# Seventeen gate/up tile pairs as seven 256-column block products instead of eight

## The reference, cut to what matters

```python
hf = rms_norm(x, norm_ffn[l])                              # 512 tokens x 1024
gate, up = jnp.split(hf @ w_ffn_in[l], 2, axis=-1)         # 1024 -> 2 x 2816
x = x + (jax.nn.silu(gate) * up) @ w_ffn_out[l]            # 2816 -> 1024
return rms_norm(x, norm_final)
```

## Time and profile before

| what | us |
|---|---|
| median of 3 runs | 1576.23 (1576.15 to 1577.49) |
| profiled execution, first to last instruction (span) | 1574.7 |
| so around the span, by the median | 1.5 |
| TensorE busy | 1565.2 (99%) |
| VectorE busy | 913.5 (58%) |
| ScalarE busy | 641.9 (41%) |
| GpSimd busy | 68.1 (4%) |
| granted TensorE clock, mean | 0.999 |

### The profile page before, as it was taken

The page is one execution under the profiler, slowest core; times in us unless marked ns, Lnnn a source line. Parts: engine busy times, 40 slices in busy tenths (PEclk is TensorE's granted clock), DMA queues, the critical chain, the costliest instruction groups (busy, mean ns, idle before and its releaser), DMA issues.

```text
span 1574.7 us, 19003 instructions
## 1 busy us (share of the span) xinstructions
PE 1565.2 (99%) x7372; PEld 1293.9 (82%) x7372; DVE 913.5 (58%) x1353; ACT 641.9 (41%) x1001; POOL 68.1 (4%) x58
## 2 busy tenths in 40 slices
PE   9999999999999999999999999999999999999998
PEld 7877777788888888888888888898888888888887
DVE  6776878666645445357787445455655544434435
ACT  5455766643222222255454334343444332222314
POOL 0000000020000000040000010010001000000002
PEclk9999999999999999999999999999999999999999
DMA  5433232343232323222221242344122332332222
GB/s 191 123 104 100 82 95 74 101 140 94 94 107 91 96 94 107 82 95 96 81 67 60 75 134 87 113 133 135 60 94 94 108 98 95 94 107 94 94 84 77
DMA packets 48522, 155.64 MB, mean 99 GB/s; under 512 B 6064, under 2 KB 7472, under 8 KB 48304
## 3 DMA queue, kind: packets, MB, share of 16 engines
q1 hardware_dynamic: 48128, 153.90, 31.0%
q10 hardware_dynamic: 304, 0.52, 0.1%
HBM read 148.11 MB, written 2.10 MB: 95 GB/s over the span
## 4 chain that ended last, share of the span: by engine, by line
PE 98%; DVE 1%; ACT 0%; DMA 0%; issue 0%; SPq 0%; DVEq 0%; ACTq 0%
PE G L1010 85%; PE SC L1010 4%; PE O L1010 2%; PE TP L1010 2%; PE M L1010 2%; PE TP L1361 1%; PE TP L1305 1%; DMA RAW<-in_va 0%; PE TP L1410 0%; DVE WL L1919 0%; ACT WH L1448 0%; DVE MGl L1919 0%; DVE RAW L2479 0%; DVE T L2193 0%; PE M L1185 0%
## 5 line engine op out<-in xcount | busy, mean ns | idle before, releaser
L1010 PE MATMUL G<-XGh,WH 128*128 128x512 f32 x1248 | 492.6, 395 | 0.0
L1010 PE MATMUL G<-XGh,WL 128*128 128x512 f32 x1248 | 486.3, 390 | 0.0
L1010 PE MATMUL G<-XGl,WH 128*128 128x512 f32 x1248 | 485.9, 389 | 0.0
L1919 DVE TENSOR_TENSOR WL<-RAW,WH 128x1024 fp32r<-128x1024 f32 (+3 forms) x281 | 337.8, 1203 | 190.8 <-ACT WH L1448 190.2
L1448 ACT ACTIVATE WH<-RAW 128x1024 fp32r<-128x1024 f32 (+3 forms) x281 | 283.8, 1011 | 185.0 <-PE G L1010 173.6
L1010 PEld LDWEIGHTS G<-XGh,WH 128*128 128x128 f32 x1248 | 234.3, 188 | 54.5 <-issue 6.2
L1010 PEld LDWEIGHTS G<-XGh,WL 128*128 128x128 f32 x1248 | 234.2, 188 | 49.8
L1010 PEld LDWEIGHTS G<-XGl,WH 128*128 128x128 f32 x1248 | 234.5, 188 | 46.4
L1010 PE MATMUL G<-MGh,WH 128*128 128x512 f32 x400 | 155.9, 390 | 0.0
L1010 PE MATMUL G<-MGl,WH 128*128 128x512 f32 x400 | 155.6, 389 | 0.0
L1010 PE MATMUL G<-MGh,WL 128*128 128x512 f32 x400 | 155.6, 389 | 0.0
(11 more groups left out here) (317 smaller groups left out, 1796.9 us busy)
## 6 DMA issues: line engine op xcount, KB each, us to landing
RAW<-in_up SPq DMA_DIRECT2D x32, 512.0 KB, 3.5
RAW<-in_dn SPq DMA_DIRECT2D x32, 512.0 KB, 3.5
RAW<-in_fg SPq DMA_DIRECT2D x22, 512.0 KB, 3.5
RAW<-in_fu SPq DMA_DIRECT2D x22, 512.0 KB, 3.5
RAW<-in_g SPq DMA_DIRECT2D x16, 512.0 KB, 3.6
RAW<-in_f SPq DMA_DIRECT2D x16, 512.0 KB, 3.5
X<-in_x SPq DMA_DIRECT2D x16, 256.0 KB, 4.1
RAW<-in_q SPq DMA_DIRECT2D x8, 512.0 KB, 3.6
```

Source lines behind the costliest of these rows:

```text
L1010: return e.matmul(dst, st, mv, start=start, stop=stop, skip_group_check=True)
L1919: return e.tensor_tensor(dst, src, hi.bitcast(F32), ALU.subtract)
```

## The change: what it does

**The block scheme.** For 17 of the 22 pairs (f = 5 to 15 and 16 to 21) gate and up are no longer two units. The pair is a product of a 2 x 2 block matrix of weights (input features 0 to 511 and 512 to 1023; gate and up) with a 2 x 2 block matrix of activations (the same halves of the features; tokens 0 to 255 and 256 to 511). Done plainly that is eight block products; done by Winograd's form of Strassen's scheme it is seven, at the price of four sums of weight blocks, four sums of activation blocks and a chain of sums of the products. Each block product is 4 chunks x 3 matmuls = 12 matmuls of 256 columns. The seven left operands are, in their order, `t1` = b11 + b12, `t2` = t1 + b22, `b11`, `t3` = b12 + b22, `b21`, `b22`, `t4` = t2 + b21.

**Weights.** The work is now counted in items, each 128x512 in hi and lo. A plain unit is two items, a pair by sevens is seven. There are 10 slots for items (the six halves of `WH`/`WL` and `WTh`/`WTl`), and items are prepared 6 ahead (`AHEAD`). VectorE makes the four weight sums (`tile_sum`) from what plain DMAs have loaded: `fg` of the pair into `RAW[f % 2]`, the two halves of `fu` into a `T` tile and a half of `RAW[2]` (`fetch`).

**Activations.** While pairs 0 to 4 still run plainly (`DIRECT`), VectorE multiplies `X` by gain and `RB` (step `h`), makes the four sums of halves (`s13`, `s2`, `s4`), and hi and lo of the sums go to `QK` (`s_hi`, `s_lo`), those of the activations to `Vh`, `Vl` (`a_hi`, `a_lo`), for each kt = 0 to 3.

**Results.** The seven products go to half banks of `O`, `M`, `TP` and `SC`; products 4, 5 and 6 (counted from 0) are added by TensorE onto the banks of 2, 0 and 3. ScalarE copies product 2 out (`one_out`), VectorE subtracts (`w_less`, `v_less`, `c22`, `c12`, `c21`), ScalarE applies Silu to the two gate halves (`c11`, `silu`), VectorE multiplies (`z_mul`), and hi and lo follow (`z_hi`, `z_lo`). Hidden tiles 8 to 15 now go to `XGh`, `XGl`.

The diff, cut to its core (the unused option of splitting on GpSimd also goes):

```diff
+DIRECT = 5
+SLOTS, AHEAD = 10, 6
+SUM_AT = (0, 1, 2, 5)
...
+    for f in range(DIRECT):
+        t += plain("fg", f, 1024) + plain("fu", f, 1024)
+    t += [("st", f, j, S) for f in range(DIRECT, 16) for j in range(7)]
+    for n in range(8):
+        t += plain("f0", n, 1024)
+    t += [("st", f, j, S) for f in range(16, 22) for j in range(7)]
...
+            if name == "st" and part == 0:
+                side = n % 2
+                behind = self.item_of["st", n - 2, 6] + 1 if ("st", n - 2, 6) in self.item_of else 0
+                new = n - 2 < DIRECT or n in (16, 17)
+                out.append(("sums", n, 2, max(behind, held.get(2, 0)) if new else behind))
+                out.append(("pair", n, side, max(behind, held.get(side, 0))))
...
+    def prepare(self, upto):
+        while self.rounded < min(upto, len(self.items)):
+            name, f, j, _ = self.items[self.rounded]
+            if name == "st" and j in SUM_AT:
+                if (f, j) == (DIRECT, 0):
+                    self.settle(self.rounded)
+                self.put("tile_sum", f, SUM_AT.index(j))
+            self.put("item_hi", self.rounded)
+            self.rounded += 1
+    def settle(self, upto):
+        while self.rest < min(upto, self.rounded):
+            self.put("item_lo", self.rest)
+            self.rest += 1
+            self.fetch()
+    def item(self, name, n, part):
+        q = self.item_of[name, n, part]
+        self.prepare(q + AHEAD + 1)
+        self.settle(q + AHEAD)
+        return q
...
+    def seven(self, f):
+        for j in range(7):
+            self.tick()
+            if j == 0:
+                for n, kind in ((3, "one_out"), (3, "w_less"), (3, "v_less"), (4, "c22"), (5, "c11"), (6, "c12"), (7, "c21"),
+                                (8, "silu"), (9, "z_mul"), (10, "z_hi"), (11, "z_lo")):
+                    self.later(n, kind, f)
+            self.put("seventh", f, j, self.item("st", f, j))
...
     def ffn(self):
...
+        for f in range(DIRECT):
             if f == 0:
...
+                for kt in range(4):
+                    for kind in ("h", "s13", "s2", "s4"):
+                        self.later(3 + 3 * kt, kind, kt)
+                    self.later(4 + 3 * kt, "s_hi", kt)
+                    self.later(4 + 3 * kt, "s_lo", kt)
+                    self.later(5 + 3 * kt, "a_hi", kt)
+                    self.later(5 + 3 * kt, "a_lo", kt)
+            self.pair(f)
+        for f in range(DIRECT, 16):
+            self.seven(f)
+        self.drain()
+        self.residuals("f0", range(8))
...
+                elif kind == "seventh":
...
+                    bank = (OM[n % 2], TP[:, 0, :], SC[:, n % 2, :], TP[:, 1, :], SC[:, n % 2, :], OM[n % 2], TP[:, 1, :])[j]
...
+                    elif j == 4:
+                        e.wait_ge(seven_act, SEVEN_ACT["one_out", pairs[n]])
+                    elif j == 5:
+                        e.wait_ge(seven_dve, SEVEN_DVE["v_less", pairs[n]])
+                    else:
+                        e.wait_ge(seven_dve, SEVEN_DVE["c22", pairs[n]])
+                    e.wait_ge(i_hi, q + 1)
+                    for kt in range(4):
+                        at = slice(kt * P, (kt + 1) * P)
+                        hi, lo = left_of[j](kt)
...
+                        mm(bank, wh[:, at], hi, start=(kt == 0 and j < 4))
+                        mm(bank, wh[:, at], lo)
+                        if kt == 0:
+                            e.wait_ge(i_lo, q + 1)
+                        t = mm(bank, wl[:, at], hi, stop=(kt == 3))
+                    t.then_inc(i_done, 1)
...
+                elif kind == "w_less":
...
+                    e.wait_ge(seven_act, SEVEN_ACT["one_out", f])
+                    e.wait_ge(i_done, taken("st", f, 1))
+                    e.tensor_tensor(W_LESS, TP[:, 0, 0:HALF_S], ONE_OUT, ALU.subtract).then_inc(seven_dve, 1)
```

More of the change, by code:

```diff
@@ L143, in __init__ @@
         self.taken, self.split, self.loaded = 0, 0, 0
+        self.items = tail()
+        self.item_of = {(name, n, part): q for q, (name, n, part, _) in enumerate(self.items)}
+        self.rounded, self.rest, self.fetched = 0, 0, 0
+        self.fetches, self.pairs = self.tail_loads(), [f for f in range(22) if ("st", f, 0) in self.item_of]
         self.chains, self.emitted = [], set()
@@ L191, in drain, with tail_loads @@
             self.tick()
+    def tail_loads(self):
+        out, held, n_plain, last_pair = [], {}, 0, 0
+        for q, (name, n, part, _) in enumerate(self.items):
+            if name == "st" and part == 0:
[4 more added lines that the diff above has]
+                out.append(("pair", n, side, max(behind, held.get(side, 0))))
+                held[side] = q + 7
+                last_pair = q + 7
+            elif name != "st" and part == 0:
+                third = (len(self.units) + n_plain) % NRAW if name in ("fg", "fu") else n % NRAW
+                out.append((name, n, third, max(held.get(third, 0), last_pair if third == 2 else 0)))
+                held[third] = q + 2
+                n_plain += 1
+        return out
     def load(self):
@@ L205, in take @@
         assert self.units[u][:2] == (name, i), (self.units[u], name, i)
-        while self.split < min(u + ahead, len(self.units)):
+        while self.split < u + ahead:
             self.split_one()
@@ L235, in gemm @@
             self.pool_product(beside, 1)
-        while self.split < min(u + NW, len(self.units)):
+        while self.split < u + NW:
             self.split_one()
@@ L581, in half_gemm @@
         if half == 0:
[L582 to L585, removed]
+            self.item("f2", n, 1)
+        self.put("mm_half", n, g, half)
         self.put(*step)
@@ L630, in ffn @@
         assert self.taken == len(self.units)
+        assert self.rest == len(self.items) and self.fetched == len(self.fetches)
     def tally(self, *kinds, each=1, but=()):
@@ L912, in program, with taken @@
         s_silu, u_done, ff_hi, ff_lo = sem("s_silu"), sem("u_done"), sem("ff_hi"), sem("ff_lo")
-        FU = tally("fu")
+        FU = {step[1]: n for step, n in tally("fu", "z_mul").items()}
+        i_hi, i_lo, i_done = sem("i_hi"), sem("i_lo"), sem("i_done")
+        d_b12, d_b22 = d_x[0:2], d_x[2:4]
+        X_LOAD = 32
+        prep_act, prep_dve, seven_act, seven_dve, t_sum = (sem(n) for n in (
+            "prep_act", "prep_dve", "seven_act", "seven_dve", "t_sum"))
+        PREP_ACT, PREP_DVE = tally("s_hi", "a_hi"), tally("h", "s13", "s2", "s4", "s_lo", "a_lo")
+        SEVEN_ACT, SEVEN_DVE = tally("one_out", "c11", "silu"), tally("w_less", "v_less", "c22", "c12", "c21")
+        TURN7 = {f: k for k, f in enumerate(pairs)}
+        RAW_LOADS, n = {}, [sum(1 for v in range(len(units)) if v % NRAW == third) for third in range(NRAW)]
+        for i, (name, _, third, _) in enumerate(fetches):
+            if name != "sums":
+                n[third] += 1
+                RAW_LOADS[name, fetches[i][1]] = n[third]
+        def taken(name, n, part=1):
+            return item_of[name, n, part] + 1
         fh_done, fh_sq, fh_acc, out_done = sem("fh_done"), sem("fh_sq"), sem("fh_acc"), sem("out_done")
@@ L1883, in _ @@
                 kind, arg = step[0], step[1:]
[L1884 to L1891 removed]
+                if kind == "sq" and arg[1] > 0 and arg not in ADDS:
                     acc, sqs = STAT[arg[0]]
@@ L1936, in _ @@
                 kind, arg = step[0], step[1:]
-                if kind == "split" and lo_of[arg[0]][0] is w_lo_dve:
+                if kind == "split":
                     v = arg[0]
```

416 lines of the change are left out of this document (351 added, 65 removed).

## The result

| | before | after |
|---|---|---|
| median of 8 runs, us | 1576.22 | 1580.45 |
| lowest to highest, us | 1575.54 to 1577.49 | 1579.59 to 1581.15 |
| profiled execution: its span, us | 1574.7 | 1578.3 (its time 1580.13) |
| mean granted TensorE clock | 0.998 to 0.999 | 0.996 to 0.997 |

The ratio is 1.0026, with a 95% interval of 1.0016 to 1.0037: the change makes the kernel slower by 4.2 us, a little more than the 0.2% that can be told here. The forecast was 1577.0, called no change that can be told, with a range of 1565 to 1588: the time lies in the range, 3.4 us above the forecast, and on the slower side of what was called no change.

A forecast was written before the change was run, and what follows sets the result against it. TensorE, busy for 99% of the span, was taken to bound the kernel. From 1574.7, minus 14.0 saved, plus 13.8 preparation and 1.0 steady part, gave 1575.5; with 1.5 around the span 1577.0, range 1565 to 1588.

The forecast's parts named there:

- TensorE's term: Matmuls of the 17 pairs by sevens: 10.06 us a pair instead of 10.88, saving 14.0 us.
- The steady part: VectorE's 18 instructions per round by sevens just fit under TensorE's 10.06 us; 1 us lost over 17 pairs.
- the rival of VectorE's pace: Rounds by sevens: waits stretch VectorE's 18 instructions to 10.5 us, giving 1583.5 us; chance 0.22.
- that of the full duration: VectorE instructions cost their full shown durations: 11.0 us a pair, 21 in the preparation, 1599 us; chance 0.05.
- The preparation: VectorE's queue from pair 0 to pair 5's `v_less`: 51.8 us plus 13.9 of waits, TensorE loses 13.8.
- the lower bound of 4 us: Preparation in pairs 0 to 5: only the round trips of the product's lo part remain, a loss of 4.
- the rival of a hidden preparation: Preparation in pairs 0 to 5 is mostly hidden and costs some 4 us, giving 1566; chance 0.22.
- the 14 us of idle time that were to show it: Sign in the trace: TensorE idle between about 1226 and 1280 for some 14 us.
- slower matmuls have 1.7 us of slack at product 5: Pair 4 stalls may lower TensorE's clock, but 1.7 us of slack at pair 5's product 5 absorbs slower matmuls.
- The rival built on it (1581): Clock falls in the preparation's stalls: 10 us at half speed beyond the slack, up to 5 more, 1581; chance 0.06.
- while VectorE is on time: Condition on ScalarE's hand-overs in a round by sevens: `one_out`, `v_less` and `c22` meet their deadlines if VectorE is on time.
- no cost taken: Second block's preparation beside `f0`, block ends and the tail were priced at nothing.

The follow-up runs named there:

- e1: Changed kernel with the last two plain units' raw buffer thirds swapped, so the load ahead of `t1` is issued earlier; 1575.66 us.
- e2: Changed kernel with ScalarE's `s_hi` of kt = 2 and `a_hi` of kt = 3 ahead of the Silus of pairs 2 and 3; 1577.22 us.
- e3: Changed kernel with the preparation's eight lo parts (`s_lo`, `a_lo`) computed on 64 columns instead of 1024, the rest left out; 1574.04 us.
- e4: Changed kernel with ScalarE's rounding of the next tile of `f0` and `f1` behind `one_out` of pairs 15 and 21; 1579.07 us.
- e9: Changed kernel with `one_out` of pair 5 ahead of the rounding of pair 6's `t2` on ScalarE; 1580.78 us.
- e11: As e10, seven plain pairs with `one_out`, `w_less` and `v_less` moved earlier, but preparation steps every 5 ticks; 1566.95 us.
- e6: Changed kernel with seven plain pairs, preparation steps every 6 ticks, the early load and e4's order at the block ends; 1567.74 us.
- e7: Changed kernel with six plain pairs, preparation steps every 4 ticks, the early load and e4's order at the block ends; 1569.11 us.
- e8: Changed kernel with eight plain pairs, preparation steps every 6 ticks and e4's order at the block ends; 1567.21 us.
- e10: e6 with, for the first pair by sevens, `one_out` ahead of the next `t2` rounding and `w_less`, `v_less` ahead of the next `t3`; 1567.03 us.
- e12: e7 with `one_out`, `w_less` and `v_less` of the first pair by sevens moved earlier as in e10; 1568.75 us.
- e5: Changed kernel with the edits of e1, e2 and e4 together; 1571.32 us.

## Why the prediction came out as it did

**TensorE's term was right.** Block products take 1.44 us and rounds 10.08, against 10.06. 17 pairs save 17 x (10.88 - 10.08) = 13.6 us instead of 14.0. That narrow matmuls eat two fifths of "one product less in eight" could be read in the earlier trace rows.

**The steady part was right, with no loss instead of 1 us.** VectorE's instructions of 512 columns start 0.60 us apart, `t1`, `t2` and `z_mul` with their waits among them. From VectorE's timeline of the changed kernel:

```profile
1285.46 0.68 DVE L2814 TENSOR_TENSOR T<-RAW,T 128x512 f32<-128x512 f32 x1
1286.06 0.69 DVE L2239 TENSOR_TENSOR WTl<-F,WTh 128x512 fp32r<-128x512 f32 x1
1286.66 0.68 DVE L2818 TENSOR_TENSOR F<-T,RAW 128x512 f32<-128x512 f32 x1
```

Waits that are already met cost nothing in this stream. This refutes the rival of VectorE's pace (10.5 us a round) and that of the full duration (11.0). The section of the Trainium skill that the second of these drew on ("VectorE: DVE Perf Modes", section "The DRAIN you can't avoid") goes on to say that an instruction which is not held starts earlier. That half of it agrees with the 0.60 us here; the rival had taken the other.

**The preparation: the queue was right, what TensorE does beside it was not.** The trace has the 61, 8 and 10 instructions of the count. The queue was to take 65.7 us, to the end of `v_less` of pair 5 at 1280.2; it took 66.9 (1214.59 to 1281.46). Most of the difference is VectorE's wait of 0.86 us for the slow bank. The load ahead of `t1` was 3.77 against 3.7 to 3.9, `s_lo` of kt = 2 1.64 against 1.8. e1 and e2 show that the load and the order on ScalarE each count with about their length, e3 that the queue's own work does once its new waits are taken off. So the lower bound of 4 us, and with it the rival of a hidden preparation, is out.

That TensorE's single waits look much like the forecast (1.0, 2.9, 0.4, 3.2, 4.6 and 1.7 at product 5 against 0.79, 2.67, none, 1.73, 4.21, and 1.22 at product 4) is in part luck. e4 runs the same instructions and has 2.97 and 2.51 for the last two in pair 4. Only their sum hangs on the queue.

Product 4 of pair 5 would have started at 1264.9 unstalled and starts at 1280.43: 15.5 us, where 13.8 were forecast. From start to start of TensorE's matmuls this is: 10.6 marked as idle; 3.35 in the two units at half clock (7.19 and 7.04 us for 5.44); 0.8 in five waits that are each 0.16 longer than marked, since the matmul ahead is shown for that long beyond its place in a stream; 0.4 in the units behind the waits of 0.79 and 1.73 us (5.62 us each); and 0.4 at the start of pair 2, the 0.1 of the forecast. For the 14 us of idle time that were to show it, 10.6 are marked. At product 5, where the forecast took its 13.8, the loss is 15.6 (1281.97 for 1266.3): VectorE is 1.3 later than forecast, and product 5 starts 0.5 behind `v_less`, because product 4 had waited for `one_out`.

**The step that failed is a sentence beside the forecast:** "since VectorE is what is late just then, slower matmuls have 1.7 us of slack at product 5". They had less, and not there. Between the slow unit and product 5 stands VectorE's reading of the bank that this unit fills. VectorE came to it at 1272.7, when 0.7 of the 1.6 us were used up, and waited for the other 0.86 (1273.58); from then on that delay was in the queue. The Trainium skill's warning of idle gaps between bursts ("TensorE: Matmul & The Clock Gate", section "Why this matters for your kernels") was to the point: the granted clock was 0.50 after the waits of 2.67 and 4.21 us. It was 1.00 after the one of 2.69 us in e4, so a gap did not always cost the clock here. The rival built on it (1581) was nearer to the time than the forecast and still not what happened: it wanted 10 us at half speed and up to 5 more; there were some 7 us, and they cost 0.9. By its own sum it would also be 1582, 1577.0 and 5.

Beside it a condition broke that the forecast had named. Each hand-over of ScalarE was to hold "while VectorE is on time", and `one_out` was given 0.6 to 1.1 us behind product 2; with VectorE late it took 2.5 us until it started, and that is the 0.5 us at product 5. e9 removed this gate alone and found VectorE's behind it.

**The term that was missing** is the end of a block, "no cost taken". I had asked whether VectorE and TensorE meet there, and not what stands ahead of `one_out` on ScalarE. The two waits at product 4 of pairs 15 and 21 are 0.3 and 0.7 us as marked and 1.5 together from start to start; e4 shows 1.4.

The sum with what was measured, from start to start: 1574.7 - 13.6 + 15.5 + 1.5, 0.1 for product 4 itself (1.54 us for 1.44) and 0.1 up to the second unit of pair 0, is 1578.3, the span. The forecast had 1575.5 for it: 1.7 too little for the preparation, 1.5 for the ends, 0.4 too much saving and the small ones, against 1.0 for a loss in the steady part that did not come. The last 0.3 us up to the time is the piece around the span. Wherever time and span are both on record they are 1.8 to 1.9 us apart (1580.13 and 1578.3), not 1.5, which came from a median and the span of a single execution.

**What stays open:** what delays the unmarked starts that cost e11 some 1.4 us; how the 1 to 3 us by which e6, e7, e8, e10 and e12 missed their forecasts are made up; why the clock fell after some waits and not after others (below). Spreading the steps over more pairs with five plain pairs was not tried, since pair 5's own weight sums need the tiles.

## What to carry to other kernels

A cheaper inner round that spends another engine's spare time is paid for at its start: count the queue of that engine between the last old round and the first new one, with each of its own waits, against what the bound engine takes for the same rounds. Here a preparation that filled its engine's queue exactly turned every hand-over, late load and step out of order into the kernel's time, 13.6 us of gain and some 17.5 of loss; two more plain rounds, more distance between the steps and a better order gave up 1.6 us of the gain and brought back 15 of the loss. Where a wait has two gates that open within a microsecond of each other, mend both before judging either.

## What the runs showed of the hardware

- The granted clock did not follow the length of the wait alone. After 2.67 us of idle time in the changed kernel it was 0.50; after 2.69 us at the same place in e4, with the same instructions up to there, it stayed at 1.00, and so it did after 2.67 us there in e9. The first row below is the changed kernel (length, busy times of PE, PEld, DVE, ACT and POOL, granted clock, DMA share, GB/s), the second e4, TensorE alone.

```profile
1236.00:1247.00 11.00, 8.33 (x30) 6.41 (x29) 9.26 (x14) 4.28 (x7) 0.00 (x0) 0.84 0.14 48
```
```profile
1236.00:1247.00 11.00, 8.30 (x37) 1.00 0.13 48
```

- It fell too after waits of 4.21, 3.19 (e3), 2.97 (e1, e4), 2.74 (e2), 2.51 (e4), 2.36 (e9) and 1.7 us (e6), and stayed at full after 2.13 (e5) and 1.73 (changed kernel). In e1 and e6 it fell only 1.7 to 1.9 us after TensorE had resumed.
- Once fallen, it cost about the same each time, 1.5 to 1.75 us of TensorE's time (7.04 and 7.19 us for a unit of 5.44, 1.5 us in e6): some 3.5 us at half speed.
- A VectorE instruction whose waits are all met, and which does not need the one directly ahead, starts 0.60 us behind one of 512 columns and 0.34 behind one of 256, while they are shown for 0.69 and 0.42; so it was in the ten rounds from pair 6 on.
